# A two-layer diffusion block with attention, convolution and sixteen experts on one core: one modulation product moved from the first layer's attention to the second's, and two common stops taken apart

## The chip, the cores and the metric

The kernel runs on one core of a Trainium2 chip. A core has TensorE (PE in the rows; PEld is its weight load), VectorE (DVE), ScalarE (ACT), GpSimd (POOL) and SyncE (SP), which run their own instruction streams and meet only through semaphores, and 16 DMA engines that they share. The metric is the device time of one execution in microseconds. All arithmetic is float32.

## The reference

There are 256 latent tokens and 256 context tokens of width 1024 and two layers. Each layer does the following, and in the second (last) one the context is only read:

```
mod  = silu(c)  @ w_ada[l] + b_ada[l]      # 1024 x 6144, six rows of 1024 for the latent
modc = silu(cc) @ w_ada[l] + b_ada[l]      # the same for the context
h    = rmsnorm(x, g_mix) * (1 + mod[1]) + mod[0]
o    = differential attention, windowed attention, convolution of h @ w_in
x    = x + mod[2] * (o @ w_out)
h2   = rmsnorm(x, g_ffn) * (1 + mod[4]) + mod[3]
y    = 2 of 16 experts for each token (router on h2)
x    = x + mod[5] * y
```

What the change moves is a third of one of these modulation products: rows 4 and 5 of the second layer's `mod`, the scale of `h2` and the gate of `y`. They are first needed when the second layer's `h2` is made.

## The kernel before

**Stages of a layer.** Each layer is written as five stages, and all engines meet at their ends. A common stop is `barrier`: the engine drains, adds one to the semaphore `phase`, and waits until the four computing engines have done so; `bar(l, k)` is the number of stop k of layer l.

1. Norm and columns, up to stop 1: VectorE scales the four tiles of 128 tokens into `YS`; TensorE transposes them in eight pieces `("nT", l, q)` (q 0 to 3 latent, 4 to 7 context, two of the eight blocks of 128 channels in each); VectorE takes the even and ScalarE the odd pieces out of PSUM and modulates them into `HT`. Transposes and evictions need the columns `AB`, which in layer one come from the product of quad (0, 0).
2. Input products, up to stop 2: `in_jobs` lists "uc" (convolution), "ka", "b", "va", "qa"; each job is eight steps k over the channels of `HT`. VectorE does the 31 convolution taps, the rope and the layer norm beside them.
3. Attention, up to stop 3: `attention_steps` writes the order by hand, for 24 units (a tile of queries and one head or pair of heads) in layer one and 12 in layer two. In a unit TensorE makes scores ("S", two units ahead), transposes the probabilities ("T") and multiplies by the values ("O"). Between them go steps of dense products: three for each unit in layer one and four in layer two (`per_unit`), as long as the list `dense` has some that may run. "A" is an eighth of a modulation quad, "W" an eighth of a half of the output product. "W" of a tile may run only when that tile's heads are mixed ("M").
4. Output product of the last tile, residual, `h2`, router, slots, up to stop 4.
5. The expert loop, up to stop 5, with weights streamed by SyncE.

**Modulation quads.** `w_ada` of a layer is cut in three quads of 2048 columns, (l, 0) to (l, 2), each four loads of 2 MB and eight steps of four matmuls (`ada_part`). Quad (0, 0) is made first of all, (0, 1) and (0, 2) among the input products, (1, 0) and (1, 2) in the first attention, and (1, 1), called `LATE`, at the start of layer two. VectorE adds the bias (`mod_rows`), GpSimd loads the bias beforehand (`load_bias`), stores rows to memory (`store_mod`) and loads them back spread over all partitions (`load_ffn_rows`, two rows for `h2` and the gain).

**Loads.** SyncE works through one list, `front_units` and then the experts, in order. Weights go into a ring of six 2 MB slots (three more while the experts run); a load waits until the unit six places earlier has been consumed. The first expert's three loads and the first load of the second fill slots during the attention; in layer one the load after that waits until all `h2` tiles are made (`h2_done`).

Of the kernel before, what the change touches and what calls it, by code (L numbers as in the profile page):

```python
# [117 lines left out]

SUMS_AFTER = {("va", 0): "mu", ("va", 2): "var"}


def bank_plan():
# [12 lines left out]
    put(("c",))  # L135
    for l in range(DEPTH):
# [3 lines left out]
        for g in range(8):  # L140
            if l == 0 and g == 4:
                for key in (("par",), ("cw",), ("ada", 0, 0), ("modc", 0)):
                    put(key)
            put(("nT", l, g), range(8 if l == 0 else 7))
# [114 lines left out]
def attention_steps(l):  # L259
# [4 lines left out]
    dense = ([("A", q) for q in range(QUADS) if q != LATE[1]] if l == 0 else []) + [("W", i, h) for i in range(nq - 1) for h in range(OUT_N)]  # L264
# [41 lines left out]
def hybrid_moe_kernel(nc, A):  # L306
# [4 lines left out]
    with ctx:  # L311
# [170 lines left out]
        bias_in = sems("bias_in", 2)  # L482
# [93 lines left out]
        def bar(l, k):  # L576
            return 5 * l + k
# [6 lines left out]
        MODS = [(l, q) for l in range(DEPTH) for q in range(QUADS) if (l, q) != LATE] + [LATE]  # L584
# [139 lines left out]
        def _(pool):  # L724
# [23 lines left out]
            def load_bias(n):  # L748

                l_, q = MODS[n]  # L750
                for j in range(4):
                    col = (4 * q + j) * CHUNK
                    pool.dma_start(bias_of(n)[32 * j:32 * j + 32, :],
                                   A["b_ada"][l_:l_ + 1, col:col + CHUNK].broadcast_to([32, CHUNK])).then_inc(bias_in[n % 2], 16)
# [18 lines left out]
            for l in range(DEPTH):  # L773
# [10 lines left out]
                barrier(pool, bar(l, 1))  # L784
# [15 lines left out]
                for q in range(1, QUADS):  # L800
                    pool.wait_ge(mod_out[l, q], 64)
                if l == 0:
                    load_bias(QUADS)
                for cnd in range(conds):
                    pool.dma_start(gate[:, cnd], modD[l, cnd:cnd + 1, 2 * D:3 * D].broadcast_to([P, D])).then_inc(gate_in[l], 16)
                if l == 0:
                    pool.wait_ge(mod_sb, QUADS + 1)
                    load_bias(QUADS + 1)
                else:
                    load_ffn_rows(l)  # L810
                for i in range(nq):
                    if l == 0 and i == 1:
                        pool.wait_ge(mod_sb, QUADS + 2)
                        store_mod(QUADS + 1)
                        pool.wait_ge(ab_done, 2)
                        pool.wait_ge(mod_out[1, 2], 64)
# [3 lines left out]
                barrier(pool, bar(l, 3))  # L820
                link(g.memset(xg[:], 0.0))

                for i in range(nq):
                    pool.wait_ge(ss2[l], i + 1)
                    rsqrt(rstd[:, i:i + 1], ss[:, i:i + 1], ms[:, i:i + 1], D).then_inc(rs2[l], 1)

# [60 lines left out]
        def _(act):  # L887
# [8 lines left out]
            for l in range(DEPTH):  # L896
# [10 lines left out]
                for q in range(1, 8, 2):  # L907
# [7 lines left out]
                barrier(act, bar(l, 1))  # L915
# [121 lines left out]
                barrier(act, bar(l, 3))  # L1037
# [63 lines left out]
        def _(dve):  # L1101
# [23 lines left out]
            def mod_rows(key):  # L1125
# [3 lines left out]
                dve.wait_ge(bias_in[n % 2], 64 * (n // 2 + 1))  # L1129
# [18 lines left out]
            for l in range(DEPTH):  # L1148
# [13 lines left out]
                for q in range(0, 8, 2):  # L1162
# [9 lines left out]
                barrier(dve, bar(l, 1))  # L1172
# [224 lines left out]
                barrier(dve, bar(l, 3))  # L1397
# [226 lines left out]
        def _(pe):  # L1624
# [26 lines left out]
            def ada_part(l, q, k):  # L1651

                key = ("ada", l, q)
                row = l if (l, q) == LATE else 0
# [18 lines left out]
            for l in range(DEPTH):  # L1673
# [5 lines left out]
                for q in range(8):  # L1679
                    if q % 4 == 0:  # L1680

                        pe.wait_ge(y_done, TILES * l + 2 + q // 2)
                    if l == 0 and q == 4:
# [12 lines left out]
                barrier(pe, bar(l, 1))  # L1696
# [25 lines left out]
                for x_, job in enumerate(jobs):  # L1722
# [11 lines left out]
                    for k in range(KD if not by_column(job) else 0):  # L1734
                        if seg == "uc":
# [83 lines left out]
                barrier(pe, bar(l, 3))  # L1819
# [164 lines left out]
```

## Time and profile before

| | us |
|---|---|
| time before, median of 3 runs | 1197.14 (1196.6 to 1198.26) |
| profiled execution, its own time | 1197.05 |
| span in that execution | 1195.3 |
| TensorE busy in the span | 965.3 |
| VectorE busy | 463.2 |
| ScalarE busy | 253.4 |
| GpSimd busy | 223.8 |
| mean granted TensorE clock, share of full speed | 0.906 |

The span runs from the first to the last instruction; the 1.75 us between it and the execution's own time lie around it. All positions below are microseconds from the start of the span. Layer one takes the span up to about 688, layer two the rest.

### The profile page before, as it was taken

What the parts mean: (1) busy time and instruction counts of PE and PEld (TensorE: products, weight loads), DVE (VectorE), ACT (ScalarE), POOL (GpSimd) and SP (SyncE); (2) the same over time, 40 slices, a digit from 0 to 9 for tenths busy, and PEclk for the clock granted to TensorE, in tenths of its full rate; (3) what the DMA queues carried; (4) which work ended last, traced back from release to release, by engine and by line L of the source; (5) the groups of instructions that cost most, each with busy time, mean ns of one, the idle gap of its engine ahead of it and who ended that gap; (6) DMA issues with size and microseconds to landing.
All of it is one profiled execution on the core that took longest, in us unless ns stands there. A gap on an engine that the chain in (4) does not pass through costs nothing. (4 is left out here: it accounts for less than half of the span.)

```text
span 1195.3 us, 23583 instructions
## 1 busy us (share of the span) xinstructions
PE 965.3 (81%) x8608; PEld 542.7 (45%) x8609; DVE 463.2 (39%) x1008; ACT 253.4 (21%) x491; POOL 223.8 (19%) x364
## 2 busy tenths in 40 slices
PE   3899999988888499999988649998887389755791
PEld 1346446455445255555544326643654244323350
DVE  1168506554535433333322176606733423211223
ACT  2100111443322022222222020113521012111120
POOL 2100000110011133343333340000000123211232
PEclk9899999999988599999999879999997589877896
DMA  9976612970004659999999796115006399999993
GB/s 370 390 311 252 275 36 85 384 293 1 1 1 192 279 205 376 412 377 424 421 415 419 310 392 253 71 71 211 2 1 274 125 384 421 412 422 421 410 410 133
DMA packets 52653, 317.94 MB, mean 266 GB/s; under 512 B 6888, under 2 KB 6968, under 8 KB 30064
## 3 DMA queue, kind: packets, MB, share of 16 engines
q1 hardware_dynamic: 40144, 284.70, 59.1%
q0 software_dynamic: 9344, 20.54, 4.7%
q10 hardware_dynamic: 3104, 11.86, 2.6%
q8 instruction: 42, 0.69, 0.2%
q14 instruction: 19, 0.16, 0.0%
HBM read 309.13 MB, written 12.65 MB: 269 GB/s over the span
## 5 line engine op out<-in xcount | busy, mean ns | idle before, releaser
L1628 PE MATMUL ps<-ring,area 128*32 128x256 f32 x3936 | 247.1, 402 | 42.8 <-DMA ring<-in_w 32.9
L1628 PE MATMUL ps<-ring,HT 128*128 128x512 f32 (+1 forms) x576 | 256.7, 598 | 8.4 <-DVEq L567 5.3
L1628 PE MATMUL ps<-area 128*32 128x256 f32 (+5 forms) x1896 | 216.6, 391 | 26.1 <-DVE area L1536 11.4
L1628 PEld LDWEIGHTS ps<-ring,area 128*32 128x32 f32 x3936 | 132.0, 115 | 130.0 <-issue 45.5
L1628 PEld LDWEIGHTS ps<-ring,HT 128*128 128x128 f32 x576 | 109.4, 195 | 137.1 <-issue 130.5
L1628 PEld LDWEIGHTS ps<-area 128*32 128x32 f32 (+2 forms) x1896 | 120.3, 136 | 50.0 <-issue 15.6
L1554 DVE COPY area<-ps 128x256 f32<-128x256 f32 x65 | 27.6, 425 | 256.2 <-PE ps L1878 256.2
L853 POOL DMA_INDIRECT expert_rows<-area x64 | 65.6, 1026 | 270.2 <-DVE area L1576 134.0
L1628 PE MATMUL ps<-HT,area 128*32 128x256 f32 x704 | 88.1, 405 | 26.7 <-DMA area<-in_w 21.4
L1082 ACT ACTIVATE area<-ps 64x256 f32<-64x256 f32 x63 | 23.8, 377 | 376.5 <-PE ps L1628 376.5
L843 POOL DMA_INDIRECT area<-h_rows,area x68 | 71.2, 1047 | 116.8 <-DVEq L567 60.7
L1628 PE MATMUL ps<-HT,ring 128*128 128x256 f32 (+1 forms) x320 | 87.3, 433 | 4.8 <-POOLq L567 3.7
L1082 ACT ACT_TABLE_LOAD x63 | 80.8, 1283 | 38.4 <-DVEq L1547 37.3
L1628 PEld LDWEIGHTS ps<-HT,ring 128*128 128x128 f32 x320 | 61.9, 196 | 27.9 <-issue 15.8
L1628 PEld LDWEIGHTS ps<-HT,area 128*32 128x32 f32 x704 | 46.5, 117 | 56.1 <-issue 33.1
L1187 DVE SCALAR_TENSOR_TENSOR area<-area,CW 128x512 f32<-128x512 f32 (+1 forms) x120 | 68.8, 614 | 3.9
L1628 PE MATMUL ps<-ring,SC 128*32 128x512 f32 x384 | 48.9, 652 | 25.9 <-DMA ring<-in_w_ada 17.6
L1576 DVE COPY area<-ps 128x256 f32 (+1 forms) x63 | 26.7, 424 | 89.9 <-PE ps L1628 55.2
L740 POOL TENSOR_SCALAR ms<-ss 128x1 f32<-128x1 f32 (+1 forms) x22 | 12.1, 551 | 227.8 <-DVE ss L1344 165.5
L1016 ACT ACTIVATE area<-ps 128x512 f32<-128x512 f32 (+1 forms) x48 | 25.2, 526 | 104.0 <-PE ps L1798 69.3
L1582 DVE SCALAR_TENSOR_TENSOR area<-area,ps 64x256 f32<-64x256 f32 x63 | 43.2, 685 | 2.0
L1306 DVE TENSOR_REDUCE mx<-ps 128x2 f32<-128x1024 f32 (+1 forms) x36 | 37.6, 1044 | 15.6 <-PE ps L1628 15.2
(197 smaller groups left out, 752.4 us busy)
## 6 DMA issues: line engine op xcount, KB each, us to landing
ring<-in_w SPq DMA_DIRECT2D x66, 2048.0 KB, 10.3
ring<-in_w_ada SPq DMA_DIRECT2D x24, 2048.0 KB, 19.0
ring<-in_w_in SPq DMA_DIRECT2D x10, 2048.0 KB, 20.9
HT<-in_w SPq DMA_DIRECT2D x10, 2048.0 KB
area<-in_w SPq DMA_DIRECT2D x10, 2048.0 KB, 10.6
area<-in_w SPq DMA_DIRECT2D x20, 1024.0 KB, 9.4
ring<-in_w_out SPq DMA_DIRECT2D x4, 2048.0 KB, 16.1
area<-expert_rows ACTq DMA_DIRECT2D x6, 1024.0 KB, 9.3
```

Of the source, the lines that this page charges most:

```text
L740: link(g.tensor_scalar(m_, s_, 1.0 / n, EPS, ALU.mult, ALU.add))
L843: pool.indirect_dma_start(xg[:, r * NW:(r + 1) * NW], None, h2_rows, bass.IndirectOffsetOnAxis(ap=at_, axis=0), bounds_check=routed(l) * N ...
L853: pool.indirect_dma_start(y_rows, bass.IndirectOffsetOnAxis(ap=sidx[r], axis=0), ym[:, r * NW:(r + 1) * NW], None, bounds_check=2 * routed ...
L1016: taken(s.activation(aT[:, k % 2, 0:kw], bank(key)[:, 0:kw], ACT.Identity), key)
L1082: s.activation(sg[0:64, :], ps[0:64, B_W13, 0:NW], ACT.Silu).then_inc(si_rdy[l], 1)
L1187: v.scalar_tensor_tensor(dst, src, w, dst, ALU.mult, ALU.add)
L1306: v.tensor_reduce(mx[:, b], pair[:, :, 0:kw], AX.X, ALU.max)
L1554: v.tensor_copy(xT.rearrange("p a s -> p (a s)"), ps[:, B_XT, 0:NW]).then_inc(xt_rdy[l], 1)
L1576: v.tensor_copy(ym[:, bass.ds(m % 2 * NW, NW)], ps[:, B_W2, 0:NW]).then_inc(y_rdy[l], 1)
L1582: v.scalar_tensor_tensor(gg[0:64, :].rearrange("s (c p) -> s p c", c=NCH), sg[0:64, :].rearrange("s (p c) -> s p c", c=NCH), TW[0:64, bass ...
L1628: return t_.matmul(out, lhsT, rhs, start=first, stop=last_)
```

## The change

- Quad (1, 2) leaves the first attention. Its four loads go from the list of layer one to that of layer two, ahead of the output weights, and its eight steps become the first entry of `dense` in the second attention. Its bias load, store and reload go along on GpSimd. `MODS`, the order of the quads, is now (0, 0) to (1, 2) in sequence, and the bias semaphores are three.
- Stop 1 goes. The eight transposed pieces are made in the order of `COLUMNS` (0, 4, 1, 5, ...), VectorE takes out pieces 0 to 3 and ScalarE 4 to 7, and the first input job waits, before its steps k = 0, 2, 4 and 6, for the one latent and the one context piece that it reads. The PSUM banks of these pieces are fixed anew. GpSimd has no wait left ahead of its padding and the bias loads of quads (0, 1) and (0, 2).
- Stop 3 goes. VectorE drains, GpSimd clears `xg` behind its first `rsqrt` of the stage instead of ahead of it, and TensorE and ScalarE go on.

```diff
+COLUMNS = (0, 4, 1, 5, 2, 6, 3, 7)
...
     if l == 0:
-        out += [("ada", 1, 4 * q + j) for q in range(QUADS) if q != LATE[1] for j in range(4)]
+        out += [("ada", 1, j) for j in range(4)]
+    else:
+        out += [("ada", 1, 4 * 2 + j) for j in range(4)]
     return out + [("out", h) for h in range(OUT_N)]
...
-    dense = ([("A", q) for q in range(QUADS) if q != LATE[1]] if l == 0 else []) + [("W", i, h) for i in range(nq - 1) for h in range(OUT_N)]
+    dense = [("A", 0 if l == 0 else 2)] + [("W", i, h) for i in range(nq - 1) for h in range(OUT_N)]
...
         def bar(l, k):
-            return 5 * l + k
+            return 3 * l + {2: 1, 4: 2, 5: 3, 6: 4}[k]
...
                         rsqrt(rstd[:, i:i + 1], ss[:, i:i + 1], ms[:, i:i + 1], D).then_inc(rs_done, 1)
-                barrier(pool, bar(l, 1))
...
                 for q in range(1, QUADS):
-                    pool.wait_ge(mod_out[l, q], 64)
-                if l == 0:
-                    load_bias(QUADS)
+                    if (l, q) != (1, 2):
+                        pool.wait_ge(mod_out[l, q], 64)
+                load_bias(MODS.index((1, 0) if l == 0 else (1, 2)))
...
-                if l == 0:
-                    pool.wait_ge(mod_sb, QUADS + 1)
-                    load_bias(QUADS + 1)
-                else:
+                if l:
+                    n = MODS.index((1, 2))
+                    pool.wait_ge(mod_sb, n + 1)
+                    store_mod(n)
+                    pool.wait_ge(mod_out[1, 2], 64)
                     load_ffn_rows(l)
...
-                barrier(pool, bar(l, 3))
-                link(g.memset(xg[:], 0.0))
...
-                for q in range(1, 8, 2):
+                for q in range(4, 8):
                     key = ("nT", l, q)
                     wait_made(act, key)
...
-                barrier(act, bar(l, 3))
...
-                for q in range(0, 8, 2):
+                for q in range(4):
...
-                barrier(dve, bar(l, 3))
+                dve.drain()
...
-                for q in range(8):
-                    if q % 4 == 0:
+                for j, q in enumerate(COLUMNS):
+                    if j < 2:
 
                         pe.wait_ge(y_done, TILES * l + 2 + q // 2)
...
-                barrier(pe, bar(l, 1))
...
                     for k in range(KD if not by_column(job) else 0):
+                        if x_ == 0 and k % 2 == 0:
+
+                            wait_taken(pe, ("nT", l, k // 2))
+                            wait_taken(pe, ("nT", l, 4 + k // 2))
...
-                barrier(pe, bar(l, 3))
```

In the following pieces, `ring,SC` is a modulation quad (four matmuls are one step), `area 128x512` the scores of a unit, `cst 128x128` its mask, L1798 a unit's transposes, and `area 128x128` a unit's products with the values.

TensorE in the first attention, units two to five, before:

```order
L1628 MATMUL ps<-ring,SC 32x512 x8
L1798 MATMUL ps<-cst,area 128x128 x4
L1628 MATMUL ps<-area 128x128 x4
L1628 MATMUL ps<-area 128x512 x2
L1628 MATMUL ps<-cst 128x128 x2
L1628 MATMUL ps<-ring,SC 32x512 x12
L1798 MATMUL ps<-cst,area 128x128 x4
L1628 MATMUL ps<-area 128x128 x4
L1628 MATMUL ps<-area 128x512 x2
L1628 MATMUL ps<-ring,SC 32x512 x12
L1798 MATMUL ps<-cst,area 128x128 x8
```

and now:

```order
L1625 MATMUL ps<-ring,SC 32x512 x8
L1798 MATMUL ps<-cst,area 128x128 x4
L1625 MATMUL ps<-area 128x128 x4
L1625 MATMUL ps<-area 128x512 x2
L1625 MATMUL ps<-cst 128x128 x2
L1798 MATMUL ps<-cst,area 128x128 x4
L1625 MATMUL ps<-area 128x128 x4
L1625 MATMUL ps<-area 128x512 x2
L1798 MATMUL ps<-cst,area 128x128 x8
```

Units three, four and five have lost their three, three and two steps of quad (1, 2); nothing has moved up into their place.

TensorE at the start of the second attention, before:

```order
L1628 MATMUL ps<-area 128x512 x6
L1798 MATMUL ps<-cst,area 128x128 x4
L1628 MATMUL ps<-area 128x512 x2
L1798 MATMUL ps<-cst,area 128x128 x4
L1628 MATMUL ps<-area 128x128 x4
```

and now:

```order
L1625 MATMUL ps<-area 128x512 x6
L1625 MATMUL ps<-ring,SC 32x512 x16
L1798 MATMUL ps<-cst,area 128x128 x4
L1625 MATMUL ps<-area 128x512 x2
L1625 MATMUL ps<-ring,SC 32x512 x16
L1798 MATMUL ps<-cst,area 128x128 x4
L1625 MATMUL ps<-area 128x128 x4
```

Four steps stand ahead of the transposes of each of the first two units.

TensorE at stop 1 of layer one, with the semaphores that it waits for (L1693 and L1690 are the transposed pieces, `HT,ring` the first input job), before:

```order
L1648 MATMUL ps<-cst,gate 128x128 [waits bank_evicted_0,mod_rows_made]
L1693 MATMUL ps<-cst,area 128x128 [waits bank_evicted_3]
L1693 MATMUL ps<-cst,area 128x128 x3
L1693 MATMUL ps<-cst,area 128x128 [waits bank_evicted_4]
L1693 MATMUL ps<-cst,area 128x128 x3
L1628 MATMUL ps<-HT,ring 128x512 [waits bank_evicted_5,ring_full_4,phase]
L1628 MATMUL ps<-HT,ring 128x512 x7
```

and now:

```order
L1645 MATMUL ps<-cst,gate 128x128 [waits mod_rows_made]
L1690 MATMUL ps<-cst,area 128x128 [waits bank_evicted_7]
L1690 MATMUL ps<-cst,area 128x128 x3
L1625 MATMUL ps<-HT,ring 128x512 [waits bank_evicted_0,bank_evicted_1,ring_full_4]
L1625 MATMUL ps<-HT,ring 128x512
L1625 MATMUL ps<-HT,ring 128x512 [waits bank_evicted_3,bank_evicted_2]
L1625 MATMUL ps<-HT,ring 128x512
L1625 MATMUL ps<-HT,ring 128x512 [waits bank_evicted_5,bank_evicted_4]
L1625 MATMUL ps<-HT,ring 128x512
L1625 MATMUL ps<-HT,ring 128x512 [waits bank_evicted_7,bank_evicted_6]
L1625 MATMUL ps<-HT,ring 128x512
```

The first input job no longer waits for `phase`; it waits in four places for two banks each. The last four transposed pieces go to banks 4 to 7 instead of 1 to 4, which the first four pieces occupied.

## Rows read from the trace of the kernel before

**Rows 1.** The stage table; each pair is busy us and (instructions), then clock, DMA, GB/s.

```profile
43.00:206.00 163.00, 160.93 (x552) 82.13 (x551) 80.73 (x109) 17.80 (x36) 7.71 (x16) 0.99 0.54 210
206.00:351.00 145.00, 126.97 (x650) 70.23 (x651) 70.42 (x174) 48.94 (x151) 14.69 (x27) 0.94 0.38 146
385.00:688.00 303.00, 257.53 (x3972) 144.10 (x3972) 93.45 (x265) 64.76 (x78) 102.62 (x164) 0.93 0.90 364
712.00:826.00 114.00, 110.94 (x356) 65.63 (x356) 52.61 (x107) 15.35 (x31) 2.29 (x6) 0.99 0.40 145
826.00:893.00 67.00, 57.22 (x300) 36.73 (x300) 36.73 (x82) 28.70 (x76) 4.61 (x8) 0.95 0.13 53
```

**Rows 2.** Timeline of TensorE, layer one to the first input jobs; start us, us, [idle].

```profile
36.06 0.66 PE L1648 MATMUL ps<-cst,gate 128*128 128x128 f32 x4 [0.86 <-DVEq L1134]
38.34 3.05 PE L1693 MATMUL ps<-cst,area 128*128 128x128 f32 x16 [1.62 <-DVE HT L1167]
42.53 29.37 PE L1628 MATMUL ps<-HT,ring 128*128 128x512 f32 x64 [1.15 <-ACTq L567]
```

**Rows 3.** The DMA view of the first 80 us.

```profile
q0 software_dynamic: 384, 0.79, 2.9%
...
area<-in_b_ada POOLq DMA_DIRECT2D x12, 64.0 KB, 7.3
```

**Rows 4.** Timeline of TensorE, first attention, units one to five.

```profile
219.56 0.66 PE L1798 MATMUL ps<-cst,area 128*128 128x128 f32 x4
...
224.96 0.63 PE L1798 MATMUL ps<-cst,area 128*128 128x128 f32 x4 [0.29 <-issue]
...
228.11 2.78 PE L1628 MATMUL ps<-ring,SC 128*32 128x512 f32 x24
...
241.35 1.06 PE L1798 MATMUL ps<-cst,area 128*128 128x128 f32 x8 [0.38 <-issue]
```

**Rows 5.** Timeline of TensorE, second attention, units nought to five.

```profile
830.80 2.00 PE L1628 MATMUL ps<-area 64*128 64x512 f32 x4 [2.46 <-ACT area L999]
832.73 1.11 PE L1798 MATMUL ps<-cst,area 128*128 128x128 f32 x4
...
835.62 0.66 PE L1798 MATMUL ps<-cst,area 128*128 128x128 f32 x4 [0.45 <-DVE area L1324]
...
838.80 0.66 PE L1798 MATMUL ps<-cst,area 128*128 128x128 f32 x4
...
847.50 1.09 PE L1798 MATMUL ps<-cst,area 128*128 128x128 f32 x8
```

**Rows 6.** Timeline of TensorE, layer two, first input jobs.

```profile
711.90 15.53 PE L1628 MATMUL ps<-HT,ring 128*128 128x256 f32 x64 [3.70 <-POOLq L567]
727.69 13.97 PE L1628 MATMUL ps<-ring,HT 128*128 128x512 f32 x32 [0.26 <-issue]
```

**Rows 7.** Timeline of VectorE, layer two, the fourth tile normed.

```profile
704.77 0.75 DVE L1157 TENSOR_SCALAR area<-X,rstd 128x1024 f32<-128x1024 f32 x1 [0.72 <-POOL rstd L741]
```

**Rows 8.** Timeline of TensorE, layer one, behind stop 3.

```profile
354.85 7.13 PE L1628 MATMUL ps<-ring,HT 128*128 128x512 f32 x16 [3.43 <-DVEq L567]
```

**Rows 9.** Timeline of ScalarE, layer one, last mixed heads taken out.

```profile
351.82 0.38 ACT L1024 ACTIVATE HT<-ps 128x256 f32<-128x256 f32 x1
```

**Rows 10.** Timeline of TensorE, layer two, behind stop 3.

```profile
895.04 8.83 PE L1628 MATMUL ps<-ring,HT 128*128 128x512 f32 x16 [1.89 <-DVEq L567]
904.33 7.11 PE L1628 MATMUL ps<-ring,HT 128*128 128x512 f32 x16 [0.46 <-issue]
```

**Rows 11.** Timeline of ScalarE, layer two, last mixed heads taken out.

```profile
893.55 0.38 ACT L1024 ACTIVATE HT<-ps 128x256 f32<-128x256 f32 x1
```

**Rows 12.** The waits of SyncE: us in total, times, longest.

```profile
SPq L573 <- DVE area L1406: 140.1, 1, 140.1
```

**Rows 13.** Timeline of SyncE, second attention and router.

```profile
822.83 81.51 SPq L706 DMA_DIRECT2D ring<-in_w  x2
911.57 0.38 SPq L708 DMA_DIRECT2D ring<-in_w  x1
```

More of the change, by code:

```diff
@@ L133, in put @@
         uses[bank] += 1
-    put(("c",))
+    put(("c",), bank=0)
     for l in range(DEPTH):
@@ L139, in bank_plan @@
             put(("ada",) + LATE, bank=7)
[L140 to L144, printed above, removed]
+        for j, q in enumerate(COLUMNS):
+            if l == 0 and j == 4:
+                for b, key in enumerate((("par",), ("cw",), ("ada", 0, 0), ("modc", 0))):
+                    put(key, bank=4 + b)
+            put(("nT", l, q), bank=j % (8 if l == 0 else 7))
+        turn[tuple(range(8))] = l
         prev = None
@@ L481, in hybrid_moe_kernel @@
         c_in = sem("c_in")
-        bias_in = sems("bias_in", 2)
+        bias_in = sems("bias_in", 3)
         mod_sb = sem("mod_rows_made")
@@ L581, in hybrid_moe_kernel @@
         ones = cst[:, C_ONE:C_ONE + P]
-        MODS = [(l, q) for l in range(DEPTH) for q in range(QUADS) if (l, q) != LATE] + [LATE]
+        MODS = [(l, q) for l in range(DEPTH) for q in range(QUADS)]
         def bias_of(n):
@@ L753, in load_bias @@
                     pool.dma_start(bias_of(n)[32 * j:32 * j + 32, :],
-                                   A["b_ada"][l_:l_ + 1, col:col + CHUNK].broadcast_to([32, CHUNK])).then_inc(bias_in[n % 2], 16)
+                                   A["b_ada"][l_:l_ + 1, col:col + CHUNK].broadcast_to([32, CHUNK])).then_inc(bias_in[n % 3], 16)
             def store_mod(n):
@@ L825, in _ @@
                     rsqrt(rstd[:, i:i + 1], ss[:, i:i + 1], ms[:, i:i + 1], D).then_inc(rs2[l], 1)
+                    if i == 0:
+                        link(g.memset(xg[:], 0.0))
                 pass_barrier(bar(l, 4))
@@ L914, in _ @@
                     taken(last, key)
-                barrier(act, bar(l, 1))
                 staged = [j for j in in_jobs(l) if is_staged(j)]
@@ L1128, in mod_rows @@
                 wait_made(dve, ("ada",) + key)
-                dve.wait_ge(bias_in[n % 2], 64 * (n // 2 + 1))
+                dve.wait_ge(bias_in[n % 3], 64 * (n // 3 + 1))
                 if key == (0, 2):
@@ L1171, in _ @@
                     mod_rows(LATE)
-                barrier(dve, bar(l, 1))
                 staged = [j for j in in_jobs(l) if is_staged(j)]
@@ L1653, in ada_part @@
                 key = ("ada", l, q)
-                row = l if (l, q) == LATE else 0
+                row = 1 if l and q else 0
                 x = slot(row, ("ada", l, 4 * q + k // 2))
@@ L1678, in _ @@
                     ada(*LATE)
-                for q in range(8):
-                    if q % 4 == 0:
+                for j, q in enumerate(COLUMNS):
+                    if j < 2:
                         pe.wait_ge(y_done, TILES * l + 2 + q // 2)
-                    if l == 0 and q == 4:
+                    if l == 0 and j == 4:
                         parameters()
```

3 lines of the change are left out of this document (removed).

## The prediction

> **What bounds the kernel.** I read the stage table first [rows 1], to see in which stretches TensorE leaves nothing idle. From 43 to 206, the input products of layer one, it is busy 160.9 of 163 us at a clock of 0.99, and from 712 to 826 (layer two) 110.9 of 114. So whatever lets these stretches start earlier is kept to their end. In the attentions it is busy 127.0 of 145 and 57.2 of 67 us, so a product put there may be free or may cost all of itself; that must be read unit by unit. From 385 to 688, the experts, the DMA engines are busy 0.90 of the time at 364 GB/s. There a saving counts only if the stream of expert weights starts earlier too. SyncE shows that it does in layer one: it waits once for 140.1 us for the last `h2` tile before it issues the second expert's first load [rows 12]. In layer two it stands 81.5 us between two expert loads, until the first half of the output product gives back its slot, and the next one goes at 911.57, behind the second half [rows 13]. Both gates move with TensorE's stages, so I count a microsecond gained before either router as a microsecond gained at the end.
>
> Then I read the timelines at each place that the change touches, and ask what is late next.
>
> **Stop 1, layer one.** Now the last transposes of the modulation columns end at 36.06 + 0.66 = 36.7, the context pieces start at 38.34 because they wait for banks that VectorE must first empty, take 3.05 us, and the first input job starts at 42.53, after another 1.15 us idle behind ScalarE's drain [rows 2]. With the pieces in banks 4 to 7 they can start at 36.8 and end at 39.8, and the job can follow at once: the evictions of four pairs, one on each of two engines, are at most one pair behind, and the job's eighth step is far behind its first. That is 2.7 us.
>
> Against it stands what GpSimd does. Stop 1 held eight bias loads back until after 42; now they go out at about 20, into the time when the loads of quad (0, 0) set the pace. In the first 80 us queue 0 used 2.9% of the 16 engines for 12 such loads [rows 3]: 0.029 x 80 = 2.3 us, eight of twelve are 1.5 us. They land about 7.3 us after issue, thus before the quad does. I take the whole 1.5 us as lost and keep 1.2 us; the bounds are the full 2.7, and -0.4 if they cost twice their own time. The Trainium skill ("DMA: Bandwidth & Descriptors", Queues, rings and completion order) says that a DMA engine goes round the queues that have work, packet by packet, so a short queue cannot be put behind a long one; by that rule the 1.5 us is paid, and by a strict first come, first served the quad's loads, issued earlier, would pay nothing and the sum would be 1.5 us better.
>
> The clock adds something. The four input jobs of "uc" take 29.37 us here [rows 2], while a block of 32 such records takes 13.97 us elsewhere [rows 6], so 29.37 - 2 x 13.97 = 1.4 us goes to half clock at its start. With TensorE at work since 38 instead of pausing twice, I take half of it back, 0.7 us (bounds 0 and 1.4). Together **-1.9 us**.
>
> **Stop 1, layer two.** The transposes end at 711.90 - 3.70 = 708.2 and the job starts at 711.90 [rows 6]. The 3.70 us are the last evictions, VectorE's rows of quad (1, 1), the drain and the stop. Without it the job waits for its first pair only, long made. But the second piece is now a context piece and waits for the fourth tile, ready at 704.77 + 0.75 = 705.5 [rows 7], while the first piece ends near 704.9: 0.6 us lost. So 3.70 - 0.3 - 0.6 = 2.8 us. The job's block took 15.53 us where its like takes 13.97 [rows 6]; it follows the longest pause, and I take these 1.5 us back as well. **-4.3 us** (bounds -2.0 and -4.5). Its weights are no bar: their load is the next one behind the quad's, and 2 MB take some 6 us at the 364 GB/s of [rows 1], against 8 us from the start of the quad's last steps to 708.9 (no row shows when it lands; if late, by 1 to 2 us, which the lower bound holds).
>
> **Quad (1, 2) out of the first attention.** Its eight steps are 24, 24 and 16 records in units three to five; 24 take 2.78 us, so a step is 0.93 us and the quad 7.4 us [rows 4]. Is it in a gap or on the path? The second attention has the same units, of the same shapes, without dense steps. From the transposes of unit two to those of unit five it takes 847.50 - 838.80 = 8.7 us [rows 5], the first takes 241.35 - 224.96 = 16.4 us [rows 4]. The difference is **-7.7 us**: the steps are fully exposed, since without them a unit already has TensorE, VectorE and ScalarE in a tight ring of about 2.9 us. The bound on the other side is -5.0, the same with one more fall of the clock. Nothing else fills the units: "W" waits for mixed heads in both versions. VectorE's bias addition goes with it. Four 2 MB loads leave a stretch where loads are not late, which is worth nothing. GpSimd no longer stores these rows in layer one.
>
> **Quad (1, 2) into the second attention.** Four steps, 3.7 us, stand ahead of the transposes of each of units nought and one. Unit nought: the scores at 830.80 take about 1.0 us at full clock (2.00 at half), the steps follow, and the transposes come at 835.6 instead of 832.73 [rows 5]: +2.9. Unit one: 0.7 + 1.0 + 3.7 = 5.4 instead of 835.62 - 832.73 = 2.9: +2.5. Together **+5.4 us**. Below stands 0, as 67 - 57.2 = 9.8 us of that stretch is idle [rows 1]; above 9.1, all 7.4 plus a fall of the clock of 1.7, from 8.83 against 7.11 us for the same 16 records [rows 10]. I stay near the unit count, since the same way of reading gives the 7.7 above. Units nought and one have a little slack, the later ones none.
>
> What else moves with it: VectorE's addition waits for a bias that GpSimd issues right behind stop 2, near 827, and needs it near 841, behind unit one's steps; at 7.3 us to land [rows 3] it is there. GpSimd then waits for the sum, stores the rows and waits again until they land, to about 849 at the same 7.3 us. Queued behind that are the reload and the first `rsqrt` of the heads, whose squares cannot come before unit five's transposes at 847.5 + 5.4 = 853. The reloaded rows are read only at the attention's end, near 893. On SyncE four loads go between "qa" and the output weights. The quad's slots come free in its own steps, so the four expert loads that used to be issued before 823 [rows 13] now go at 833 to 843. The DMA engines are nearly empty in that stretch, 53 GB/s from 826 to 893 [rows 1]: 8.4 MB at 364 GB/s take 23 us of 67, so this is hidden and costs nothing.
>
> **Stop 3.** Layer one: TensorE starts the last tile's product at 354.85 after 3.43 us idle [rows 8]; it needs only the mixed heads, out at 351.82 + 0.38 = 352.2 [rows 9]. The rest is VectorE's residual and its scaling of two rows. **-2.5 us** (bounds -1.2, -2.6). Behind it the squares, GpSimd's `rsqrt` and `h2` start as much earlier, and the last residual follows TensorE. Layer two: 895.04 against 893.55 + 0.38 = 893.9 [rows 10, 11], **-1.0 us**; if the shorter pause also spares the slow start, up to 1.7 more, so 0 to -2.7.
>
> **Sum.** -1.9 - 7.7 - 2.5 - 4.3 + 5.4 - 1.0 = -12.0 us, against the profiled execution's own 1197.05: 1185.05. The median before is 0.1 higher, so I predict **1185.1**.
>
> **Rivals.**
> - *The clock takes its share.* The fill kept TensorE busy in units that now have small pauses, and the four steps may meet the slow stretch that stands at 830.80 [rows 5]. With one fall of 1.7 us more in each attention and neither slow start regained (0.7 + 1.5), 5.6 us go: 1190.7. For it: clocks of 0.94 and 0.95 in the attentions, 0.99 in the dense stretches [rows 1]. Against it: in the bare units two to five of the second attention TensorE has pauses below half a microsecond. The Trainium skill ("TensorE: Matmul & The Clock Gate", The HAM clock gate) says that activity releases the throttle and idleness brings it back; by that rule removing the fill could cost, and shorter pauses at the stops gain.
> - *The stops gave nothing*, since other waits end where they ended (evictions, the gate rows). Then -7.7 + 5.4 = -2.3 us, 1194.8. Against it: the releasers of 3.70 and 3.43 us are other engines' drains, and in layer one the mixed heads were out 2.6 us before TensorE went on.
> - *More than counted.* The bias loads cost nothing, the slow starts vanish at both fronts and behind the last stop 3: -1.5 - 0.7 - 1.7, and 1 us of the quad hidden, 1180.2.
> - *Slower: the expert weights of layer two come late.* Four units more go through the ring ahead of the output weights. If the slots were not back before the output product, 8.4 MB, 23 us, would be moved into the stretch that the DMA engines bound: -12.0 + 23 = +11, 1208.1. It decides from the point where the four loads are issued later than about 890 instead of 843. The order of SyncE's list speaks against it.
>
> **Chances.** Forecast 0.60, clock 0.15, stops nothing 0.07, more 0.15, slower 0.03. Forecast's own range is 1182 to 1188.5. For eight in ten I reach into both neighbours, 1179.5 to 1191, and leave out the far end of 1194.8 and 1208. A change of 0.2%, 2.4 us, is about what this measurement can tell: the stops rival lies on that line and goes mostly to no change. Faster 0.93, same 0.04, slower 0.03.
>
> **What would show it.** After: TensorE's first input jobs start near 41.3 and have no idle row for another engine's drain; transposes of units two and five in the first attention stand 8.7 us apart; the router's last `h2` comes 12 us earlier; layer two's input jobs follow the transposes within 0.5 us; the second attention has two groups of 32 records ahead of its first two transposes and unit one takes about 5.4 us; expert loads sit in the second attention. It would be wrong if the quad's loads landed later, if an expert loop grew by what the stages before it lost, or if the bias sum waited for GpSimd.

## The result, and the profile after

The changed kernel takes 1188.88 us (median of 8 runs, 1185.95 to 1192.58). Beside it on the same chip the kernel before takes 1197.49 (8 runs, 1192.29 to 1201.6). The ratio is 0.9932 [0.9912, 0.9951]: 8.6 us faster by the medians. The profiled execution took 1186.26 us, span 1184.5, at a mean granted clock of 0.910, and stands 10.8 us below that of before. It is one draw: the runs of one kernel spread over 7 to 11 us. So a second profile of the same kernel ("again" below, 1187.51 us) stands beside it, and I read no difference of a microsecond from one pair alone.

The busy time and clock by stage, the lines that answer to [rows 1] (columns as there):

```profile
core 0: us, PE busy (x) PEld busy (x) DVE busy (x) ACT busy (x) POOL busy (x), PEclk, DMA share, GB/s
43.00:205.75 162.75, 159.73 (x552) 81.96 (x552) 84.06 (x115) 20.48 (x42) 4.00 (x8) 1.00 0.55 214
205.75:341.43 135.68, 119.31 (x583) 67.58 (x584) 68.68 (x171) 48.73 (x150) 10.67 (x19) 0.94 0.24 91
380.76:669.53 288.77, 250.64 (x3925) 140.77 (x3925) 87.20 (x237) 64.76 (x78) 100.59 (x160) 0.94 0.89 364
698.07:810.96 112.89, 109.48 (x358) 64.55 (x356) 54.05 (x110) 17.01 (x35) 2.12 (x4) 1.00 0.42 158
810.96:882.96 72.00, 63.51 (x358) 37.61 (x359) 36.84 (x82) 28.37 (x74) 8.66 (x16) 0.95 0.44 171
```

The expert stretch of layer one is as long as before and the DMA engines are as busy: what was gained ahead of it was kept behind it. The second attention moves three times the data (171 against 53 GB/s) and TensorE stays at 0.95.

From marks on TensorE's timeline in the three traces I made this table. Each line is a stretch between two such marks and the lines add up to the span:

```
stretch (us)                              before   after          again
start to first scores, layer one          206.92   205.75 (-1.2)  205.16 (-1.8)
first scores to transposes of unit 8       51.07    43.52 (-7.5)   41.89 (-9.2)
to the last mixed heads                    92.61    92.16 (-0.5)   92.45 (-0.2)
stop 3: to the last tile's product          4.25     1.74 (-2.5)    1.75 (-2.5)
to the rank product                        36.71    37.59 (+0.9)   37.50 (+0.8)
experts, to quad (1, 1)'s first steps     288.64   288.77 (+0.1)  287.79 (-0.8)
layer two, to its first scores            146.16   141.43 (-4.7)  140.83 (-5.3)
first scores to transposes of unit 2       12.44    18.39 (+6.0)   19.54 (+7.1)
to the last mixed heads                    53.48    53.61 (+0.1)   56.26 (+2.8)
stop 3: to the last tile's product          2.76     1.80 (-1.0)    1.74 (-1.0)
that product, to the first transposed h2   16.65    14.83 (-1.8)   14.92 (-1.7)
to the rank product                        22.10    22.19 (+0.1)   22.19 (+0.1)
experts, to the end                       261.51   262.72 (+1.2)  263.69 (+2.2)
sum                                      1195.30  1184.50 (-10.8) 1185.70 (-9.6)
```

**The front of layer one**, TensorE's timeline (start, us, instruction, count, idle before and what ended it), answers to [rows 2]:

```profile
31.30 1.92 PE L1625 MATMUL ps<-ring,SC 128*32 128x512 f32 x16 [2.56 <-DMA ring<-in_w_ada]
36.28 3.43 PE L1625 MATMUL ps<-ring,SC 128*32 128x512 f32 x16 [3.05 <-DMA ring<-in_w_ada]
40.55 0.66 PE L1645 MATMUL ps<-cst,gate 128*128 128x128 f32 x4 [0.84 <-DVEq L1132]
41.04 1.91 PE L1690 MATMUL ps<-cst,area 128*128 128x128 f32 x16
43.02 27.71 PE L1625 MATMUL ps<-HT,ring 128*128 128x512 f32 x64
```

The job follows its pieces without a pause, as meant, and at full clock (27.71 us for the block of 29.37 before). But it starts at 43.02, later than 42.53, since the quad's last steps wait for their load until 36.28. In the kernel before the same two waits end here:

```profile
28.29 3.20 PE L1628 MATMUL ps<-ring,SC 128*32 128x512 f32 x16 [2.83 <-DMA ring<-in_w_ada]
33.28 1.06 PE L1628 MATMUL ps<-ring,SC 128*32 128x512 f32 x8 [1.78 <-DMA ring<-in_w_ada]
```

So the loads come 3.0 us later in both places. It is no chance of one trace: in the nine profiles of kernels that send the bias loads early, the two waits end 2.7 to 3.9 us later than in the kernel before. What the DMA engines moved from 24 to 32 us, after first and then before:

```profile
DMA packets 541, 2.77 MB, mean 346 GB/s; under 512 B 144, under 2 KB 144, under 8 KB 262
```
```profile
DMA packets 427, 3.37 MB, mean 421 GB/s; under 512 B 16, under 2 KB 16, under 8 KB 16
```

**The first attention** (answers to [rows 4]) and **the second** (to [rows 5]), TensorE's timeline of the kernel after:

```profile
211.92 3.81 PE L1625 MATMUL ps<-ring,SC 128*32 128x512 f32 x24
215.66 0.66 PE L1798 MATMUL ps<-cst,area 128*128 128x128 f32 x4
...
225.41 0.63 PE L1798 MATMUL ps<-cst,area 128*128 128x128 f32 x4 [0.29 <-issue]
...
234.09 1.09 PE L1798 MATMUL ps<-cst,area 128*128 128x128 f32 x8
...
810.96 3.41 PE L1625 MATMUL ps<-area 64*128 64x512 f32 x8 [0.72 <-ACTq L571]
...
817.04 3.64 PE L1625 MATMUL ps<-ring,SC 128*32 128x512 f32 x32
820.62 0.66 PE L1798 MATMUL ps<-cst,area 128*128 128x128 f32 x4
...
822.26 3.64 PE L1625 MATMUL ps<-ring,SC 128*32 128x512 f32 x32
826.19 0.63 PE L1798 MATMUL ps<-cst,area 128*128 128x128 f32 x4 [0.29 <-issue]
```

From the transposes of unit two to those of unit five it is 8.7 us now (16.4 before). The two groups of 32 records stand where they were forecast and unit one takes 826.19 - 820.62 = 5.6 us. The 24 records that took 2.78 us before now take 3.81 in one place: half clock for a part of them.

**Stop 3 in layer one and in layer two, and the front of layer two** (answer to [rows 8], [rows 10] and [rows 6]):

```profile
341.43 0.82 PE L1817 MATMUL ps<-cst,area 128*128 128x128 f32 x6
343.17 7.11 PE L1625 MATMUL ps<-ring,HT 128*128 128x512 f32 x16 [0.92 <-ACT HT L1023]
...
698.07 13.98 PE L1625 MATMUL ps<-HT,ring 128*128 128x256 f32 x64
...
884.76 7.11 PE L1625 MATMUL ps<-ring,HT 128*128 128x512 f32 x16 [0.92 <-ACT HT L1023]
892.23 7.11 PE L1625 MATMUL ps<-ring,HT 128*128 128x512 f32 x16 [0.37 <-issue]
```

The releaser is now ScalarE's instruction that takes out the mixed heads, not another engine's drain. In layer two the first 16 records run at full clock: 7.11 us where [rows 10] has 8.83. In layer one a part of the 2.5 us is lost again: the router's 32 short records take 5.30 us (5.20 in the second profile) for 4.38 before, the +0.9 and +0.8 of the table. The job of layer two has no idle time ahead of it and takes 13.98 us for 15.53.

GpSimd and SyncE in the second attention (start, us, instruction; idle time before and its releaser), answer to [rows 13]:

```profile
827.00 1.03 POOL L765 DMA_DIRECT2D mod_rows<-area  x2 [13.22 <-DVEq L1132]
...
834.47 1.08 POOL L774 DMA_DIRECT2D X<-mod_rows  x2 [5.15 <-DMA mod_rows<-area]
...
848.23 0.19 POOL L744 TENSOR_SCALAR ms<-ss 128x4 f32<-128x4 f32 x1 [12.16 <-DVE ss L1341]
```
```profile
819.11 2.04 SPq L710 DMA_DIRECT2D ring<-in_w  x2
824.31 0.38 SPq L712 DMA_DIRECT2D ring<-in_w  x1
826.07 66.26 SPq L710 DMA_DIRECT2D ring<-in_w  x2
```

The rows are back long before VectorE scales them near 884, and GpSimd waits 12 us for the head squares behind them. The expert loads sit in the second attention and land there.

### The profile page after: what moved, and what is told of

Its sections match the earlier page's. It is cut to its first block and busy times, and to the rows that moved or that the text cites. A ratio compares the mean times of both kernels' runs of the same rounds, so it can differ in the third digit from the quotient of the medians.

```text
span 1184.5 us, 23570 instructions
## 1 busy us (share of the span) xinstructions
PE 960.2 (81%) x8608; PEld 537.7 (45%) x8609; DVE 463.5 (39%) x1008; ACT 253.0 (21%) x491; POOL 225.3 (19%) x364
## 5 line engine op out<-in xcount | busy, mean ns | idle before, releaser
L1625 PEld LDWEIGHTS ps<-ring,area 128*32 128x32 f32 x3936 | 129.2, 115 | 133.4 <-issue 45.4
L1625 PE MATMUL ps<-HT,ring 128*128 128x256 f32 (+1 forms) x320 | 84.1, 422 | 0.1
L1625 PE MATMUL ps<-ring,SC 128*32 128x512 f32 x384 | 51.7, 686 | 26.9 <-DMA ring<-in_w_ada 17.8
L757 POOL DMA_DIRECT2D area<-in_b_ada x24 | 12.6, 531 | 199.2 <-ACTq L571 109.2
L1303 DVE TENSOR_REDUCE mx<-ps 128x2 f32<-128x1024 f32 (+1 forms) x36 | 37.6, 1044 | 18.3 <-PE ps L1625 17.8
```

The lines of the kernel that those rows point to most:

```text
L757: pool.dma_start(bias_of(n)[32 * j:32 * j + 32, :], A["b_ada"][l_:l_ + 1, col:col + CHUNK].broadcast_to([32, CHUNK])).then_inc(bias_in[n % ...
L1303: v.tensor_reduce(mx[:, b], pair[:, :, 0:kw], AX.X, ALU.max)
L1625: return t_.matmul(out, lhsT, rhs, start=first, stop=last_)
```

## The experiments

Ratios are to the kernel before, run on the same chip beside them.

**The move alone.** The kernel before with the quad's part of the change only:

```
-    dense = ([("A", q) for q in range(QUADS) if q != LATE[1]] if l == 0 else []) + [("W", ...
+    dense = [("A", 0 if l == 0 else 2)] + [("W", ...
```

> The kernel before with quad (1, 2) moved and both stops kept. My theory: the first attention gives 7.7 us (transposes of unit two to those of unit five 8.7 us apart instead of 16.4), the second takes 5.4 to 6 (unit one from 2.9 to 5.6), so about 2 us faster than before, 1195. Rival (the move is what made the kernel faster, the quad is hidden in the second attention): 7 to 8 us faster, 1190. In the trace, TensorE still stands 3.4 to 3.7 us idle behind VectorE's and GpSimd's drains, and its first input job starts at 42.5.

Measured: 1197.2 us, ratio 0.9994 [0.9974, 1.0014]. Its trace has the 8.7 us between the two sets of transposes in the first attention, and 19.5 us instead of 12.4 from the first scores to unit two in the second. The first input job starts at 45.26 and not at 42.5 as expected: the quad's last load is on time (33.21), but its last steps and what follows fall on half clock (3.64 us for 1.92). So the move gives -7.7 between the two sets and +7.1: it brings at most some 3 us, and none can be told.

**The stops alone.** The changed kernel with the quad back in the first attention (the same line the other way).

> The changed kernel with quad (1, 2) back in the first attention, in the place and order of before; both stops stay away. My theory: most of the gain is here, 1.2 + 2.5 + 4.5 + 1 to 2.5 us, so 9 us faster than before in the trace, 1188. Rival (other waits take the place of the stops): within 2 us of before. The first attention has its 16.4 us from unit two to unit five again, the second its 2.9 us for unit one.

Measured: 1189.49 us, ratio 0.993 [0.9904, 0.9955]. This is all of the gain of the whole change. Stop 1 was never put back by itself; what it is worth is read from the traces alone, and what stop 3 is worth from the runs further down.

**The bias loads later.** GpSimd issues the eight early bias loads only behind quad (0, 0), when no load of a quad is waited for:

```
                 if l == 0:
+                    pool.wait_ge(mod_sb, 1)
                     load_bias(1)
                     load_bias(2)
```

> The changed kernel, in which GpSimd waits for the rows of quad (0, 0) before it issues the eight bias loads of quads (0, 1) and (0, 2). My theory: these loads delayed the quad's third and fourth load by 3.0 us (31.30 and 36.28 against 28.29 and 33.28); without them these are back at 28.3 and 33.3 and the first input job starts at about 40.0 instead of 43.0: 3 us faster than the changed kernel, if the clock does not fall there (half clock on the job's start would take back up to 1.7). Rival (something else moved the loads, the order of the first transposes or chance): they stay at 31 and 36.

Measured: 1185.66 us, ratio 0.9909 [0.9882, 0.9937]. In its trace:

```profile
23.75 6.56 PE L1626 MATMUL ps<-ring,SC 128*32 128x512 f32 x48
33.22 3.51 PE L1626 MATMUL ps<-ring,SC 128*32 128x512 f32 x16 [2.91 <-DMA ring<-in_w_ada]
37.60 0.66 PE L1646 MATMUL ps<-cst,gate 128*128 128x128 f32 x4 [0.87 <-DVEq L1133]
38.09 1.91 PE L1691 MATMUL ps<-cst,area 128*128 128x128 f32 x16
40.08 6.25 PE L1626 MATMUL ps<-HT,ring 128*128 128x512 f32 x14
```

The last load is back at 33.22, the place of before, and the first input job starts at 40.08, 2.9 us earlier than in the changed kernel. The first scores come at 202.90 (205.75), so it is kept until there. The median says the same (0.2% less), but the intervals overlap, and the profiled span is only 0.7 us shorter: the experts of layer two take 265.4 us there for 262.7.

**Half of them later.** As above, with the wait between the two calls, so that four loads go early and four late.

> The changed kernel with the four bias loads of quad (0, 1) early, as changed, and those of quad (0, 2) held until the rows of quad (0, 0) are made. Eight early loads put the third load of the quad off by 3.0 us, none by 0. Theory (each of the slow loads takes its share of the DMA engines from the quad): four put it off by 1.5 us, to 29.8, and the first input job starts at about 41.5. Rival (a fixed cost of a second queue at work): 3.0 us again, or none.

Measured: 1187.62 us, ratio 0.9924 [0.9897, 0.995]; the third load's steps start at 29.86, as expected, and the quad's last steps at 34.86. None early 33.22, four 34.86, eight 36.28: each four cost 1.4 to 1.6 us in these three traces (in the other eight with eight early the last steps start at 36.1 to 37.2). The delay goes roughly with what is sent. The first input job starts at 42.68, not at 41.5: behind the load, half clock took the rest.

**The changed kernel once more.**

> The changed kernel once more, on the chip of the other three. Expected: the ratio to the kernel before as first measured, 0.9932, within its interval; the trace differs from the first one only in where the clock falls, by up to 1.7 us in a place.

Measured: 1188.33 us (12 runs, 1186.14 to 1197.2), ratio 0.9936 [0.9912, 0.9959]. Its profile is the last column of the table above.

**The quads in TensorE's pauses.** In both attentions the eight steps leave units nought to two; three stand between the first scores, where TensorE waits for ScalarE, and five in units five to seven, where it waits for VectorE:

```
-    out = [("S", 0), ("S", 1)]
+    quad, a_k = 0 if l == 0 else 2, 3
+    out = [("S", 0), ("S", 1)] + [("A", quad, j) for j in range(a_k)]
+    a_steps = {5: 1, 6: 2, 7: 2}
...
+        out += [("A", quad, a_k + j) for j in range(a_steps.get(n, 0))]
+        a_k += a_steps.get(n, 0)
```

The column product of the context moves from unit five to eight with it, and the store and reload of quad (1, 2) behind the first head squares.

> The changed kernel with the eight steps of a quad, in both attentions, put where TensorE stands idle: three between the second and the third scores, where it waits 1.6 to 2.5 us for ScalarE, then one, two and two in units five, six and seven, where it waits 0.5 to 2.1 us for VectorE; the modulation columns follow in unit eight and GpSimd's store and reload behind the first heads. My theory (a step costs its 0.93 us in the tight units and little in a gap): both attentions get shorter by 3 to 5 us, in all 6 to 9 us faster than the changed kernel, about 1179. Rival (a step costs the same wherever it stands, since the units are a ring): no faster than the changed kernel.

Measured: 1174.4 us, ratio 0.98 [0.9767, 0.9833]. TensorE's timeline, first attention:

```profile
205.52 1.99 PE L1629 MATMUL ps<-area 64*128 64x512 f32 x8 [1.35 <-DVEq L575]
207.44 2.78 PE L1629 MATMUL ps<-ring,SC 128*32 128x512 f32 x24
210.15 1.13 PE L1629 MATMUL ps<-area 64*128 64x512 f32 x4
211.27 0.66 PE L1802 MATMUL ps<-cst,area 128*128 128x128 f32 x4
...
231.48 1.92 PE L1629 MATMUL ps<-ring,SC 128*32 128x512 f32 x16
233.34 0.66 PE L1802 MATMUL ps<-cst,area 128*128 128x128 f32 x4
```

The 2.78 us of steps at 207.44 lie where the changed kernel is idle for 2.51 us behind ScalarE. From the first scores to the transposes of unit eight it takes 37.7 us (43.5) in the first attention and 39.3 (42.9) in the second: 5.9 and 3.6 of the 10.3 us between the two profiles. In the kernel before, with no quad in it, the second takes 36.8 us. So the same 7.4 us of work costs 6.1 us there in one place and 2.5 in another. By the ratios the gain over the changed kernel is 1.3%, 16 us, more than the 6 to 9 expected and more than the pair of profiles shows; the rest I can't place, and what the column product and GpSimd's store and reload add by moving along no run tells.

**Both: pauses, and bias loads later.**

> The kernel with the quads' steps in TensorE's idle places and the eight bias loads held back until the rows of quad (0, 0) are made. If both gains are real and independent, the first input job starts near 40.0 and the attentions are as short as in the kernel with the steps in idle places: 3 us faster than that one, ratio to before 0.977. Rival (the 3 us are given back further on, in the clock or behind the input products): ratio 0.980 as without.

Measured: 1173.23 us, ratio 0.9804 [0.9769, 0.9838], span 1170.1. Its trace is the shortest of all, with the first input job at 40.45, but the ratio is the one that the rival gave, and its interval holds 0.977 as well: in the time nothing of the 2.4 us at the front can be told.

**Stop 3 restored in both layers** of the changed kernel:

```
-                dve.drain()
+                barrier(dve, bar(l, 3))
...
+                barrier(pool, bar(l, 3))
...
+                barrier(act, bar(l, 3))
...
+                barrier(pe, bar(l, 3))
```

GpSimd's clearing of `xg` goes back to its old place, right behind the stop.

> The changed kernel with stop 3 put back in both layers, all else as changed. My theory (stop 3 is worth 2.5 us in layer one and 1.0 in layer two plus what the slow start behind it costs): TensorE stands 3.4 us idle behind the last mixed heads in layer one and 1.9 in layer two, and the kernel is 3.5 to 5 us slower than the changed one. Rival (the squares and the residual behind it had slack, so only stop 1 counts): no slower than the changed kernel.

Measured: 1198.82 us, ratio 1.0014 [0.9986, 1.0043]. The whole gain was gone: three times what the two terms of the prediction, 3.5 us, had made me expect. So I ran it again, and each layer alone.

> The kernel with both common stops behind the attention restored, once more, unchanged. If its time is a property of the kernel: 1198 to 1199 us, ratio 1.000 to 1.003, layer one's stop 4.25 us and layer two's 7.7 us in the trace again. If a good part of it was chance of the chip: 1192 to 1195, and layer two's stop nearer 2.8 us.

Measured: 1201.32 us, ratio 1.0042 [1.002, 1.0063], a little above what was expected. It is the kernel, not chance. Its trace has 4.25 us and 7.70 us at the two places again, and behind the second one:

```profile
891.25 10.17 PE L1626 MATMUL ps<-ring,HT 128*128 128x512 f32 x16 [6.82 <-POOLq L571]
```

> The changed kernel with the common stop behind the attention restored in layer one only. Theory A, the stop has a cost of its own in each layer, and in layer two GpSimd comes to it late: here the way from the last mixed-heads transposes to the last tile's product is 4.25 us (with the single wait 1.74), the expert part before the ranks gives about as much again back or loses it (38 to 40 us from there to the rank product), layer two keeps its 1.80 us; so 3 to 5 us over the changed kernel, 1191.5 to 1193.5 us, ratio to the kernel before 0.996. Theory B, the 10 us of both stops together are mostly a matter of where the clock falls and of where the instructions lie in memory: then one stop alone may cost 8 us or nothing.

Measured: 1192.13 us, ratio 0.997 [0.9949, 0.999], against 0.9936 of the changed kernel: 0.34%, 4 us. The place itself takes 4.25 us instead of 1.75. Behind it, to the rank product, it is 40.2 us instead of 37.6:

```profile
345.60 8.83 PE L1633 MATMUL ps<-ring,HT 128*128 128x512 f32 x16 [3.43 <-DVEq L571]
```

That is 8.83 us for 7.11, and 0.9 more in the router's 32 records. The first kernel with both stops has the same 40.2; its repeat has 36.8, the kernel before 36.7. So a clock that falls behind the stop, or doesn't, decides over 3.4 us between two profiles of one kernel.

> The changed kernel with the common stop behind the attention restored in layer two only. Theory A (GpSimd, which has done nothing since the last head squares, is late at this stop): the way from the last mixed-heads transposes to the last product is again 7 to 8 us where the single wait gives 1.80, GpSimd's own queue is named as the releaser, and the time is 5 to 7 us over the changed kernel, about 1194.5 us, ratio 0.9975. Theory B (the place of the code, so chance): the way is 2.8 us as in the kernel before, VectorE is named, and the time is 1 to 3 us over, about 1190.5.

Measured: 1197.54 us, ratio 1.0014 [0.9993, 1.0034]: 0.78%, 9 us for this one stop, more than the 5 to 7 of theory A. TensorE's timeline around it, and what GpSimd waited for from 870 to 905 (us in total, times, longest):

```profile
882.21 0.88 PE L1825 MATMUL ps<-cst,area 128*128 128x128 f32 x6 [0.53 <-DVE area L1351]
891.14 9.53 PE L1633 MATMUL ps<-ring,HT 128*128 128x512 f32 x16 [8.05 <-POOLq L571]
901.04 7.11 PE L1633 MATMUL ps<-ring,HT 128*128 128x512 f32 x16 [0.37 <-issue]
```
```profile
POOL area L823 <- POOLq L571: 9.8, 1, 9.8
```

All four engines are let go at 891.1 by GpSimd's own queue. Yet GpSimd's last instruction before the stop ended at 881.43, and VectorE's, the last of any, at 883.67 + 1.22 = 884.9. So the stop lasts 6.2 us longer than the slowest engine's work, and behind it 16 records take 9.53 us instead of 7.11: 7.2 us of wait and 2.4 of clock. The two profiles with both stops show the same (idle 6.8 us, releaser the same, 3.1 us of clock). In the kernel before, with the same four barriers, the releaser was VectorE and the idle time 1.89 us [rows 10]. The kernel with the move alone has them too, and GpSimd's store and reload of quad (1, 2) in the second attention besides:

```profile
897.24 7.13 PE L1628 MATMUL ps<-ring,HT 128*128 128x512 f32 x16 [2.29 <-DVEq L569]
```

So the move alone doesn't make GpSimd late.

What kept GpSimd? I let it count itself at the start of the attention and not wait here:

```
+                pool.sem_inc(phase, 1)
                 for i in range(nq):
...
-                barrier(pool, bar(l, 3))
```

> Both common stops behind the attention restored, but GpSimd counts itself at the start of the attention and doesn't wait there; its clearing of the expert tile stands where the changed kernel has it. TensorE, ScalarE and VectorE stop as in the kernel before. Theory A, GpSimd's late arrival makes layer two's stop dear: the way from the last mixed-heads transposes to the last product in layer two is 2.8 to 3.5 us instead of 7.7, in layer one still 4.2, and the time is 4 us under the kernel with both stops, about 1194.5. Theory B, another engine holds it: the way stays 7.7 us, and the time about 1198.5.

Measured: 1197.33 us, ratio 0.9998 [0.9976, 1.002]. In its trace VectorE is the releaser again:

```profile
889.18 0.82 PE L1819 MATMUL ps<-cst,area 128*128 128x128 f32 x6
892.29 7.13 PE L1627 MATMUL ps<-ring,HT 128*128 128x512 f32 x16 [2.29 <-DVEq L571]
```

At the place, then, theory A held: 3.1 us instead of 7.7 to 8.9, and 16 records behind it take 7.13 us. The edit takes away both GpSimd's drain and its wait, so which of the two is late it doesn't say. The time didn't follow it all the way. It lies 0.16% and 0.44% under the two runs with GpSimd at the stop, where the 4.6 us at the place and some 3 of clock would make 0.6%; and it lies 7 us over the changed kernel, of which its two stops explain 2.5 + 1.4 us. The rest of its trace, against the second profile of the changed kernel, is 1.7 us at the front, 1.6 at the start of the first attention, 1.5 in the experts of layer one and 2.2 in those of layer two, less 0.7 ahead of the first rank product. The experts of layer two take 261.0 and 261.5 us in the two kernels that have stop 1, and 262.0 to 265.9 in the twelve profiles without it; within the twelve I see no order. Why, no run shows. I leave that part open.

Why GpSimd comes late isn't shown either. In the three traces where it does, the only transfer in that stretch is one packet of 0.02 MB on an instruction queue, between its last work and the release (stop 3 of layer two alone, from 883 to 891):

```profile
q8 instruction: 1, 0.02, 1.0%
```

It lies at 884.9, 6.2 us before the release; in the two others 5.0 us before it, and each time at the end of VectorE's last instruction. In the kernel before such a packet comes at 895.0, also at the end of VectorE's last instruction, which is there the release itself, and holds nobody. That may be a fetch of instructions that one of these engines needs before it can go on, but whose queue this is no row says, and the packet's own time, 1.0% of 16 engines over 8 us, is 1.3 us of the 5 to 6. The cause stays open.

## Why the prediction was right, and where it was not

The time, 1188.9, lies in the range of 1179.5 to 1191 and 3.8 us over the forecast, just outside the forecast's own 1182 to 1188.5. Point by point, by its steps:

- **What bounds the kernel.** Right. What was gained before either router stayed behind it: the rank product of layer one comes at 380.76 for 391.56, 10.8 us earlier, and quad (1, 1)'s first steps behind the experts at 669.53 for 680.20, 10.7; the first transposed `h2` of layer two at 899.59 for 911.69, 12.1. The expert stretch of layer two then took 1.2 to 2.2 us longer. I had written that a loop which grew by what was saved ahead of it would speak against me: here a tenth to a fifth of the saving went that way, and it is longer in all twelve profiles without stop 1.
- **Stop 1, layer one, -1.9:** measured -1.2 and -1.8. The mechanism held (with the bias loads held back the job starts 2.1 and 2.5 us earlier than before, where I had 2.7), but two sizes were off and nearly cancelled, which is luck. The eight bias loads cost 3.0 us, not 1.5: I took their own time on the engines and not what the quad's loads lost. The Trainium skill ("DMA: Bandwidth & Descriptors", Queues, rings and completion order) has the engines go round the queues packet by packet; by that rule a price is paid, and the 0, 1.6 and 3.0 us agree in kind, while first come, first served would give nought. The clock gave back 1.7 us in the first job, not 0.7.
- **Stop 1, layer two, -4.3:** -4.7 and -5.3 to the first scores. From quad (1, 1)'s first steps to the first job 28.5 us instead of 31.7, and the block 1.55 shorter. Right.
- **Quad out, -7.7:** 7.7 us between the transposes that I named; over the whole start of the attention -7.5 and -9.2. A half-clock stretch fell on other steps, 3.81 for 2.78 us. (The bound of -5.0 was not one fall of 1.7 us, which gives -6.0; nothing else hangs on it.)
- **Quad in, +5.4:** +6.0 and +7.1, in the kernel with the move alone also +7.1. The unit count held (5.6 us for unit one), the slow scores ahead of it (3.41 us, 810.96) cost the rest. This is the term that was too small in these pairs. Without the quad the stretch itself takes 12.4 us in the kernel before and 13.5 with the stops alone, so 5.4 lies within what the clock does there.
- **Stop 3, -2.5 and -1.0:** that in both traces at the place itself. Behind the one of layer two came 1.7 to 1.8 of clock, which the text had as a bound and left out of the sum; behind the one of layer one 0.8 to 0.9 was lost, so there `h2` did not come "as much earlier".
- **The rivals.** "The stops gave nothing" is refuted: they gave all of it, and the move, for which I had -2.3, gave nothing that can be told (its interval, 0.9974 to 1.0014, holds the 2.3 too). "Slower" is refuted by the expert loads in the second attention. "The clock takes its share" is true in part: the places of half clock moved, by 1 to 2.8 us each, gains at the fronts and losses in the attentions, and the median lies between this rival's 1190.7 and the forecast.

The sum read place by place, -12.0, stood at 899.59 as -12.1; the profile kept 10.8 of it and the medians 8.6. That the two agree so well is in part luck: the 1.8 us of clock that I had left out stand against 0.9 lost ahead of the first rank product, 0.7 at the first front and 0.6 with the quad. What failed is thus small: the quad's arrival and the clock. What the prediction hadn't seen is how unlike its mirror image a removed stop is. I priced it as the wait in one trace, 3.5 us for stop 3; put back into the new order it costs 9 to 13 us (0.78% and 1.06% by ratios). A part of that is shown: in layer two GpSimd is then the late engine, 4.6 us at the place and 2.4 to 3.1 of clock behind it. But without GpSimd in it the stop still costs 7 us in the time, and some 3 of them have no cause that a run shows.

## What to carry to other kernels

A common stop costs at least the wait for its latest engine, and which one that is can change with any edit: where a stop protects one buffer, wait for that buffer, and price the stop by a range, not by the wait in one trace. Work moved as filler is worth the difference of the pauses, not its own length: look for the rows with idle time and a releaser, and put the filler there (a ratio of 0.98 for 0.993 here, where moving it to another layer gave nothing). And small loads that are sent early for comfort delay the large ones that are waited for; send them behind, though here only the trace shows the 3 us, not the time.

## What the runs showed of the hardware that I had not expected

- Eight loads of 64 KB, 0.5 MB, put off 2 MB loads that were under way by 3.0 us (2.7 to 3.9 over nine profiles), though 0.5 MB at 421 GB/s are 1.3 us. From 24 to 32 us the engines moved 346 GB/s in all instead of 421.
- A stop of four engines was let go 5 to 6 us after the last engine's work, by one that had been idle for 8.5 to 9.8 us, in three profiles of three. In the two profiles of kernels that have stop 1 too, VectorE let the same stop go, after TensorE had stood idle for 1.9 and 2.3 us.
- The same instructions of the second attention take 53.6 and 56.3 us in two profiles of one kernel: 2.7 us, more than three of the six terms of my sum.
